# Row sums of squares: two fp32r products of their high and low parts in place of one fp32 matmul

## The reference

```python
def rms_norm(x, g):
    xf = x.astype(jnp.float32)
    y = xf * lax.rsqrt(jnp.mean(xf * xf, axis=-1, keepdims=True) + EPS)
    return (y * g.astype(jnp.float32)).astype(x.dtype)

def sqrelu_mlp(h, w1, w2):
    return jnp.square(jax.nn.relu(h @ w1)) @ w2

def swiglu_ffn(x, w_in, w_out):
    gate, up = jnp.split(x @ w_in, 2, axis=-1)
    return (jax.nn.silu(gate) * up) @ w_out
```

## Time and profile before

| | |
|---|---|
| time, median of 3 runs | 1545.57 us (1545.5 to 1545.82) |
| profiled execution, its own time | 1546.58 us |
| its span, first to last instruction | 1544.8 us |
| PE busy | 1532.1 us, 99% |
| VectorE busy | 1044.0 us, 68% |
| ScalarE busy | 848.9 us, 55% |
| GpSimd busy | 122.8 us, 8% |

### The profile page before, as it was taken

One profiled execution on the slowest core, in us unless ns is written; L12 is line 12 of the kernel. 1 busy time (PEld: TensorE's weight loads), 2 busy tenths in 40 slices (PEclk: granted clock), 3 DMA queues, 4 the chain that ended last, 5 costly groups with the idle time before them and its releaser, 6 DMA issues.

```text
span 1544.8 us, 35078 instructions
## 1 busy us (share of the span) xinstructions
PE 1532.1 (99%) x12812; PEld 1493.7 (97%) x12812; DVE 1044.0 (68%) x1764; ACT 848.9 (55%) x1300; POOL 122.8 (8%) x123
## 2 busy tenths in 40 slices
PE   9999999999999999999999999999999999999999
PEld 8899999988999999999999999989999988999999
DVE  7777765644876557666787766668576657687764
ACT  6776654536665445545445555556555547665543
POOL 1830000045000000000000000000000033200000
PEclk9999999999999999999999999999999999999999
DMA  7246556554566665666565555656555981066564
GB/s 249 67 131 198 192 189 205 164 172 143 192 196 197 192 192 191 194 193 204 188 210 193 196 192 193 205 184 210 191 191 191 229 212 64 15 205 192 193 201 151
DMA packets 80640, 280.53 MB, mean 182 GB/s; under 512 B 8864, under 2 KB 12448, under 8 KB 80544
## 3 DMA queue, kind: packets, MB, share of 16 engines
q1 hardware_dynamic: 76656, 274.29, 54.8%
q10 hardware_dynamic: 3888, 4.85, 1.7%
HBM read 277.53 MB, written 1.57 MB: 181 GB/s over the span
## 4 chain that ended last, share of the span: by engine, by line
PE 92%; DVE 4%; DMA 2%; ACT 1%; issue 1%; SPq 0%; DVEq 0%; ACTq 0%
PE psum L1776 27%; PE psum L1777 27%; PE psum L1780 27%; PE psum L1918 2%; PE psum L1920 2%; PE psum L1919 2%; DMA raw<-tiles 2%; PE psum L2209 1%; PE psum L2160 1%; DVE w_lo L1052 1%; ACT w_hi L578 1%; PE psum L2193 0%; PE psum L2105 0%; PE psum L1983 0%; PE psum L1973 0%
## 5 line engine op out<-in xcount | busy, mean ns | idle before, releaser
L578 ACT ACTIVATE w_hi<-raw 128x1024 fp32r<-128x1024 f32 x517 | 546.0, 1058 | 476.9 <-PE psum L1780 425.8
L1052 DVE TENSOR_TENSOR w_lo<-raw,w_hi 128x1024 fp32r<-128x1024 f32 x482 | 589.7, 1224 | 248.0 <-ACT w_hi L578 247.6
L1776 PE MATMUL psum<-xs,w_hi 128*128 128x256 f32 x1904 | 528.5, 278 | 1.0 <-DVE w_lo L1052 1.0
L1777 PE MATMUL psum<-xs,w_hi 128*128 128x256 f32 x1904 | 526.0, 276 | 0.0
L1780 PE MATMUL psum<-xs,w_lo 128*128 128x256 f32 x1904 | 526.0, 276 | 0.0
L1776 PEld LDWEIGHTS psum<-xs,w_hi 128*128 128x128 f32 x1904 | 357.4, 188 | 1.7 <-DVE w_lo L1052 1.4
L1777 PEld LDWEIGHTS psum<-xs,w_hi 128*128 128x128 f32 x1904 | 357.4, 188 | 0.2
L1780 PEld LDWEIGHTS psum<-xs,w_lo 128*128 128x128 f32 x1904 | 357.3, 188 | 0.0
L1780 PE MATMUL psum<-hs,w_lo 128*128 128x256 f32 x1280 | 353.3, 276 | 0.0
L1776 PE MATMUL psum<-hs,w_hi 128*128 128x256 f32 x1280 | 353.3, 276 | 0.0
L1777 PE MATMUL psum<-hs,w_hi 128*128 128x256 f32 x1280 | 353.3, 276 | 0.0
(11 more groups left out here) (292 smaller groups left out, 1484.1 us busy)
## 6 DMA issues: line engine op xcount, KB each, us to landing
raw<-tiles SPq DMA_DIRECT2D x517, 512.0 KB, 4.2
bias<-bias_dram ACTq DMA_DIRECT2D x8, 256.0 KB, 7.2
x<-x_in SPq DMA_DIRECT2D x4, 256.0 KB, 5.3
w1c_all<-w1c_k ACTq DMA_DIRECT2D x4, 256.0 KB, 4.3
w1c_all<-w1c_v ACTq DMA_DIRECT2D x4, 256.0 KB, 6.0
y_out<-x SPq DMA_DIRECT2D x8, 128.0 KB, 2.1
con<-consts SPq DMA_DIRECT2D x1, 803.0 KB, 8.9
bias_dram<-bias_row ACTq DMA_DIRECT2D x1, 512.0 KB, 7.1
```

Of the source, the lines that this page charges most:

```text
L578: act.activation(slot_part(w_hi[s], t + RING * q if isinstance(q, int) else t), raw[s][:, :], ACT.Copy).then_inc(hi_ready, 1)
L1052: dve.tensor_tensor(slot_part(w_lo[s], t_), raw[s][:, :], hi_of(slot_part(w_hi[s], t_)), ALU.subtract).then_inc(lo_ready, 1)
L1776: pe.matmul(out, w_hi[s][:, c:c + P], x_hi, start=first, stop=False)
L1777: pe.matmul(out, w_hi[s][:, c:c + P], x_lo, start=False, stop=False)
```

## The change

`ones` gets a copy `ones_r` in fp32r, made by VectorE at the start (128 elements more in each partition of SBUF, which moves the tensors allocated behind it by 512 bytes). `ssq_parts` takes the high and low part of `ssq`, on memory that `scratch` uses at other times. For the nine names of `TO_ROWS`, ScalarE's `root` first waits for the complete sum and copies it to fp32r, VectorE's `norm` first subtracts that copy from `ssq`, and `sums` on PE waits for both (`ssq_split`) and multiplies `ones_r` by the high part and the low part into the same bank. In `sums` the fp32 column matmuls now go ahead of the row product.

```diff
@@ sbuf and semaphores
+        with nc.sbuf_tensor("ssq_parts", [P, 2 * S], F32R) as ssq_parts:
+            pass
         scratch = sb("scratch", [P, 12 * S])
...
         ones = sb("ones", [P, P])
+        ones_r = sb("ones_r", [P, P], F32R)
...
-        ssq_ready = sem("ssq_ready")
+        ssq_ready, ssq_split = sem("ssq_ready"), sem("ssq_split")
@@ ScalarE
             def root(name):
+                if name in TO_ROWS:
+                    act.wait_ge(ssq_ready, SSQ0[name] + KD + 1)
+                    act.activation(ssq_parts[:, 0:S], ssq[:, :], ACT.Copy).then_inc(ssq_split, 1)
                 act.wait_ge(stat_done, STAT0[name])
@@ VectorE
             def norm(name):
+                if name in TO_ROWS:
+                    count = 2 * TO_ROWS.index(name)
+                    hi, lo = ssq_parts[:, 0:S], ssq_parts[:, S:]
+                    dve.wait_ge(ssq_split, count + 1)
+                    dve.tensor_tensor(lo, ssq[:, :], hi_of(hi), ALU.subtract).then_inc(ssq_split, 1)
                 dve.wait_ge(std_ready, STD0[name])
...
+            dve.wait_ge(const_ready, 1)
+            dve.tensor_copy(ones_r[:, :], ones[:, :])
             dve.wait_ge(vec_loaded, 16)
@@ TensorE, in sums(name)
-                    if name in TO_ROWS:
-                        ins = pe.matmul(bank(RB, 0, S), ones[:, :], ssq[:, :], start=True, stop=True)
                     if name in TO_COLUMNS:
                         for tb in range(TB):
                             ins = pe.matmul(bank(STAT, tb, tb + 1), ssq[:, tb * P:(tb + 1) * P], ones[:, 0:1], start=True, stop=True)
+                    if name in TO_ROWS:
+                        pe.wait_ge(ssq_split, 2 * (TO_ROWS.index(name) + 1))
+                        pe.matmul(bank(RB, 0, S), ones_r[:, :], ssq_parts[:, 0:S], start=True, stop=False)
+                        ins = pe.matmul(bank(RB, 0, S), ones_r[:, :], ssq_parts[:, S:], start=False, stop=True)
```

## The result

The changed kernel takes 1577.44 us, median of 4 runs (1576.44 to 1578.04), against 1545.69 (1545.5 to 1546.01) for the kernel before: 2.0% more, ratio 1.0200 with a 95% interval from 1.0188 to 1.0212. The profiled execution took 1577.88 us, its span 1576.0.

The account below looks back on a forecast made before the run. TensorE bounds the kernel: matmul count times start spacing, plus waits. Stalls less matmul savings gave +0.7 us, the slow beat +37.7; 1546.58 became 1585.0, less 1.0 for the median: 1584.0 us, range 1566 to 1590.

Parts of the forecast that it names:

- the beat: PE's matmul spacing, 113.3 ns fast or 117.8 slow; six stretches behind L1769 were to turn slow, +37.7 us.
- three stretches called surest: `ffn_0`, `ffn_1`, `post_1`, each following a `residual_one` that ends fast, were to turn slow: 4596 matmuls, 20.5 us.
- rival 4: `glu_2` also slow, since its turn at 1114.54 needs the mark in place: +5.3 us, 1589; chance 0.08.
- PE then reaches L1769 in the fast beat: In `two()`, with the fp32 matmul gone, the remaining filler was to turn fast to slow, at 4.45 ns per matmul.
- Rival 2: The pair turns the beat as the fp32 matmul did; PE meets L1769 slow, leaves fast: 1546.3 us; chance 0.06.
- the mark: In the slow beat, the one matmul in three lasting 280 ns where neighbours last 279; its place decides the turn.
- The signs that the forecast named: Behind `up_0`'s L1769: L1777 starts 353 ns apart, durations 279 and 280; some 1360 matmuls, not 1414, from 130 to 290 us.
- shift it: Two more fp32r matmuls move the mark off the next matmul, leaving `pre_0`, `mid_0`, `post_0` slow: 17.2 us.
- the stalls: PE waiting for the split: 1.1 us in `mix_0`, 0.55 in `pre_0`, 0.75 in `mid_0`.
- the 1.0 us that I took off: Median of runs lay 1.0 us below the profiled execution, so the forecast went from 1585.0 to 1584.0.
- rival 1: Some of `pre_0`, `mid_0`, `post_0` return to the fast beat: 1570 us if two do, other mixes 1567 to 1580; chance 0.32.
- Rival 3: One beat only, a 109.2 ns gap; L1769's turns have a cause the change leaves alone: 1546.3 us; chance 0.03.

Follow-up runs that it names:

- with constants and nothing to wait for: Kernel before, its fp32 row-sum matmul replaced by two fp32r products of ready constants, without split or new wait, row sums of squares left out: 1567.51 us.
- With constants and all stretches fast: Kernel before with a product pair of ready constants, row sums of squares left out, filler eight products behind the pair: 1543.06 us, ratio 0.9979.
- late pair with n = 7: Changed kernel with the product pair six products later and the filler seven products behind the pair: 1548.8 us, ratio 1.0009.
- three fillers: Changed kernel with two more fillers in each of seven wide stages, 7 and 13 products behind the first: 1549.15 us, ratio 1.0017.
- without a filler: Changed kernel without the one filler (L1782) behind the first paired tiles of each wide stage: 1575.48 us, one run.
- the split with the fp32 matmul: Changed kernel keeping split and wait, but with the old single fp32 matmul on unsplit squares in place of the two products: 1565.04 us, ratio 1.0121.
- With the late pair a filler at n = 1: Changed kernel with the product pair six products later and the filler one product behind the pair: 1583.28 us, ratio 1.0236.

## Why the prediction was right or wrong

**Direction and kind of loss: right.** The loss is the beat, 4.45 ns a matmul, at the same granted clock. Five slow stretches, 1530 + 1530 + 1578 + 762 + 1536 = 6936 matmuls, make 30.9 us of the 31.2 between the two spans (1576.0 and 1544.8). The three stretches called surest are slow, with 20.5 us as forecast. `glu_2` kept its turn to the fast beat (rival 4).

**The step that failed.** "PE then reaches L1769 in the fast beat, as at 101.62, and leaves it in the slow one." PE reaches it in the slow beat. "An ordinary fp32r matmul never turned the beat in thousands" holds for the stream, not for these two: with constants and nothing to wait for they turned it as well. Rival 2 had this half right and drew the wrong end from it. It said that a slow arrival leads to a fast leaving, which is true only where product n+1 is marked, and the pair put the mark on the fifth, where the fp32 matmul had put it on the fourth. The three sure stretches came out slow for another reason than the one given, so that the size of this term, 20.5 us, came out right by luck: with the pair's mark one place earlier, or the filler one product later, as an experiment shows (1548.26 us), all three are fast. The signs that the forecast named couldn't tell the two ways apart; the spacing of the six products ahead of the filler does, 117.5 ns where it took 113.3 for granted.

**The mark in `post_0`.** Carrying the mark through the pair by counting two more matmuls ("shift it", "one place past the next matmul") gave slow for all three stages that are entered slow. `post_0` is entered slow and without a stall, its marks were the fourth and the seventh, and the filler turned it fast. That is 1536 x 4.45 ns = 6.8 us and the bulk of the miss of 6.6. The other two parts nearly cancel: the stalls were 0.8 us smaller than forecast, and the 1.0 us that I took off, since the profiled execution before lay that far above its median, wasn't there after (1577.88 against 1577.44). It is one of the mixes of rival 1. In `pre_0` and `mid_0` the stall stood between the old mark and the new one, so that counting had no ground there; they came out slow, as forecast, by a mechanism that the forecast didn't have. In `pre_0` the first three products behind the pair last 280, 278 and 280 ns; with the third marked the sixth is too, and the filler at n = 6 meets the unmarked seventh.

**The stalls.** `mix_0` 1.1 forecast, 0.84 measured at the first filler of `wo_a` (its last product ahead starts at 101.32, before at 100.48). `pre_0` 0.55 and 0.35, `mid_0` 0.75 and 0.46. The last two were of the right size for PE in the fast beat (0.56 and 0.74 with the filler moved; the forecast's own terms for the two add up to 0.58 and 0.77), and smaller in the changed kernel since PE came later, from a slow stretch. `ffn_0`, `ffn_1`, `post_0` and `post_1` had none, as forecast.

**The matmul itself.** The pair's two spacings are 0.11 and 0.12 us, as forecast, against 0.443. With constants and all stretches fast the kernel takes 1543.06: 1.7 us for the pair and 0.75 for the 168 matmuls of `mix_1`'s wide stage that turned fast too make 1543.2 from 1545.67. In that session the median of the kernel before was 1546.36, but ten of its 21 runs went at a granted clock of 0.999 or 0.998; the eleven at 1.000 have a median of 1545.7, so the ratio of 0.9979 makes the gain look larger than it is. The intended gain is real, a ninth of a per cent.

**Rival 3.** It rested on the warm gap of the Trainium skill (TensorE: Matmul & The Clock Gate, Back-to-back issue gap), N/2.4 + 2.5 ns, 109.2 ns for 256 columns. The same section calls this the gap of a single isolated matmul and says that in a stream of weight loads and matmuls both set the spacing, so the formula doesn't rule a beat out, as the rival took it to. The traces show two, neither of them 109.2, and no run shows what sets them: both 113.3 and 117.8 ns stand in stretches of over 1500 matmuls at a granted clock of 1.00, here even in one kernel, behind `post_0` and ahead of it.

**No version beats the kernel before** with the row sums computed. The late pair with n = 7 comes to its 1545.5 in its four best runs, with a ratio of 1.0009 over all. Of the 1.7 us of the pair a stall in `mix_0` like that of the changed kernel takes some 0.8 and a new wait for a weight tile in `mix_1`'s stage 0.55 by the distance of starts; the rest wasn't traced to a place. The three fillers are the steadiest changed kernel, and cost 3.1 us for it.

**Open.** What in the chip keeps the beat and the mark. Why a pair of constants marks the third product and a pair of real operands the fifth; one more met wait isn't it. What decides the beat behind a stall: in `pre_0` and `mid_0` it was fast behind the late operands of the pair in four cases (`pre_0` without a filler, `mid_0` with the filler later, both with three fillers), and slow in the others. The length of the stall doesn't decide it by itself: in `mid_0` the starts ahead of the pair were 0.77 us apart both without a filler and with the filler later, and the beat was slow behind the first and fast behind the second. Why the rule fails for a filler right behind the late pair. Whether a place one full turn of the mark further on does as well (n = 9 in the kernel before) wasn't run.

One case of the split with the fp32 matmul looked like an exception: in `post_0`, entered slow, the second to fifth products lasted 282, 280, 284 and 280 ns, and the filler left it slow. The same 282, 280, 284, 280 stands in `pre_0` of the changed kernel with the filler later and in `mid_0` of the late pair with n = 7. There the filler at n = 7 turned the beat fast, which fits the fifth and the eighth as the marked ones; with n = 6 the seventh comes next, and slow is what the rule says.

## What to carry to other kernels

- Where a long stream of equal matmuls sets the time, read the distance of starts (last less first, by the count) in every stage of both kernels. The busy share, the clock and the chain were the same here at 113.3 and at 117.8 ns.
- An edit around such a stream is judged by the beat that it leaves behind, not by its own price: 0.216 us a time gained, 31 us lost; and one 60-column matmul moved by one product cost 37.5 us in the kernel before and gave back 29 in the changed one.
- A single filler is tuned to one exact sequence, and a wait or another matmul ahead of it can undo it. Three, with 7 and 6 products between them, gave the fast beat from every start seen here, for 0.44 us a stage.

## What the runs showed that I had not expected

- Two fp32r matmuls of the stream's own shape, on `ones_r` and into another bank, turned the fast beat slow, with real operands and with constants.
- A stall bears on it too, both ways, and a very short one does. In `mix_1`'s wide stage of the changed kernel the beat was fast behind the filler at 305.75 and turned slow at 311.41, with no fp32 matmul near. Timeline, PE and VectorE:

```profile
311.30 0.28 PE L1793 MATMUL psum<-xs,w_lo 128*128 128x256 f32 x1
311.41 0.33 PE L1789 MATMUL psum<-xs,w_hi 128*128 128x256 f32 x1
311.58 0.28 PE L1790 MATMUL psum<-xs,w_hi 128*128 128x256 f32 x1
...
310.10 1.21 DVE L1058 TENSOR_TENSOR w_lo<-raw,w_hi 128x1024 fp32r<-128x1024 f32 x1
```

  The next tile's low part ends at 311.31, just when PE wants it, and L1789 is that tile's first product, ahead of which PE waits for it; one distance of 0.17 in place of 0.11 is all that shows. That this wait of about 0.06 us cost the rest of the stage its beat is read from where it stands. The split with the fp32 matmul shows the same: fast up to 305.30, one distance of 0.17, then slow.
- Behind the real pair, met in the fast beat, the first mark that can be read is the fifth product's. With the late pair a filler at n = 1 left `ffn_0` slow and one at n = 7 turned it fast, although they lie two full turns of the mark apart.
